# Three passages between blocks of a two-layer transformer, worked through in halves of 256 tokens

## What is computed

```python
h = x
for layer in range(DEPTH):
    u = rmsnorm(h, mix_pre_g[layer])
    ...
        mixed = jnp.concatenate([mla_out, moba_out], axis=-1) @ ab_w_out[e]     # layer 0
    ...
        mixed = stick_breaking_attention(qkv[0], qkv[1], qkv[2]) @ sb_w_out[o]  # layer 1
    h = h + rmsnorm(mixed, mix_post_g[layer])
    u = rmsnorm(h, ffn_pre_g[layer])
    gu = u @ ffn_w_gate_up[layer]
    f = (jax.nn.silu(gu[..., :D_FF]) * gu[..., D_FF:]) @ ffn_w_down[layer]
    h = h + rmsnorm(f, ffn_post_g[layer])
```

## Time and profile before

| | |
|---|---|
| Median of 3 runs | 1420.4 us (1417.37 to 1420.62) |
| The profiled execution's own time | 1417.1 us |
| Its span | 1415.1 us |
| TensorE busy, products (PE) | 1345.1 us, 95% |
| VectorE (DVE) | 728.1 us, 51% |
| ScalarE (ACT) | 528.5 us, 37% |
| GpSimd (POOL) | 239.1 us, 17% |
| Mean granted TensorE clock | 0.974 of full |

### The profile page before, as it was taken

How to read it: one execution, slowest core, us unless ns; L and a number is a source line. 1 busy time by engine, 2 the same in 40 slices (tenths; PEclk the granted TensorE clock), 3 DMA queues, 4 the chain that set the end, 5 groups by cost and what they waited for, 6 DMA issues and landing times.

```text
span 1415.1 us, 16882 instructions
## 1 busy us (share of the span) xinstructions
PE 1345.1 (95%) x6255; PEld 1099.5 (78%) x6255; DVE 728.1 (51%) x925; ACT 528.5 (37%) x796; POOL 239.1 (17%) x156
## 2 busy tenths in 40 slices
PE   7888999988999999999888999999989999999997
PEld 5666888866888888888667888888768888888886
DVE  5777645437544544222366666655376544553223
ACT  5366655544332223222343443333433232223112
POOL 0333000013111111000111222222232111110002
PEclk9989999998999999999898999999979999999999
DMA  5321332131333333333221121120313333333331
GB/s 161 108 52 31 82 82 75 33 102 45 108 100 93 100 94 95 95 94 95 62 60 31 45 60 44 44 74 16 104 45 104 89 104 89 104 105 89 92 102 60
DMA packets 187213, 112.08 MB, mean 79 GB/s; under 512 B 8944, under 2 KB 181557, under 8 KB 187166
## 3 DMA queue, kind: packets, MB, share of 16 engines
q1 hardware_dynamic: 185356, 106.68, 25.9%
q0 software_dynamic: 640, 2.10, 0.5%
q10 hardware_dynamic: 1170, 2.66, 0.5%
HBM read 109.30 MB, written 4.74 MB: 81 GB/s over the span
## 4 chain that ended last, share of the span: by engine, by line
PE 85%; DVE 6%; ACT 3%; issue 3%; POOL 3%; DMA 0%; POOLq 0%; ACTq 0%; DVEq 0%; SPq 0%
PE banks L370 27%; PE banks L372 26%; PE banks L371 26%; PE banks L1382 3%; DVE w_lo L365 1%; POOL residual L606 1%; PE banks L1190 1%; PE banks L403 1%; DVE tf L571 1%; ACT u_hi L594 1%; ACT probsT_hi L1198 0%; DVE logits L1152 0%; PE banks L391 0%; DVE tf L1077 0%; DVE diag L421 0%
## 5 line engine op out<-in xcount | busy, mean ns | idle before, releaser
L365 DVE TENSOR_TENSOR w_lo<-w_raw,w_hi 128x1024 fp32r<-128x1024 f32 (+2 forms) x200 | 298.1, 1493 | 298.6 <-ACT w_hi L358 298.1
L370 PE MATMUL banks<-u_hi,w_hi 128*128 128x512 f32 x1040 | 417.6, 402 | 26.0 <-DVE u_lo L560 21.3
L371 PE MATMUL banks<-u_lo,w_hi 128*128 128x512 f32 x1040 | 411.0, 395 | 0.0
L372 PE MATMUL banks<-u_hi,w_lo 128*128 128x512 f32 x1040 | 410.7, 395 | 0.0
L358 ACT ACTIVATE w_hi<-w_raw 128x1024 fp32r<-128x1024 f32 (+2 forms) x200 | 206.3, 1032 | 247.3 <-PE banks L372 247.2
L370 PEld LDWEIGHTS banks<-u_hi,w_hi 128*128 128x128 f32 x1040 | 198.6, 191 | 78.6 <-issue 20.0
L372 PEld LDWEIGHTS banks<-u_hi,w_lo 128*128 128x128 f32 x1040 | 198.6, 191 | 42.5
L371 PEld LDWEIGHTS banks<-u_lo,w_hi 128*128 128x128 f32 x1040 | 199.0, 191 | 41.2 <-issue 1.0
L693 POOL TENSOR_TENSOR up<-up,gate 128x512 f32<-128x512 f32 x44 | 72.6, 1649 | 400.8 <-DVE up L717 364.0
L677 ACT ACTIVATE gate<-gate 128x512 f32<-128x512 f32 x44 | 27.9, 634 | 214.9 <-DVE gate L713 214.9
L1402 POOL TENSOR_TENSOR stick_lo<-stick,stick_hi 128x1280 fp32r<-128x1280 f32 x16 | 56.7, 3543 | 209.2 <-DVE stick_hi L1398 209.2
(11 more groups left out here) (235 smaller groups left out, 1939.1 us busy)
## 6 DMA issues: line engine op xcount, KB each, us to landing
w_raw<-in_ffn_w_gate_up_dram SPq DMA_DIRECT2D x88, 512.0 KB, 3.8
w_raw<-in_ffn_w_down_dram SPq DMA_DIRECT2D x30, 512.0 KB, 3.6
w_raw<-in_sb_w_qkv_dram SPq DMA_DIRECT2D x24, 512.0 KB, 3.9
w_raw<-in_ab_w_in_dram SPq DMA_DIRECT2D x17, 512.0 KB, 3.9
w_raw<-in_ffn_w_down_dram SPq DMA_DIRECT2D x16, 448.0 KB, 3.6
w_raw<-in_ab_w_out_dram SPq DMA_DIRECT2D x8, 512.0 KB, 3.9
w_raw<-in_sb_w_out_dram SPq DMA_DIRECT2D x8, 512.0 KB, 4.1
bias_by_distance<-bias_rows ACTq DMA_DIRECT2D x1, 2560.0 KB
```

The lines of the kernel that those rows point to most:

```text
L365: dve.tensor_tensor(wl[:, c.slot, 0:w], raw[:, c.slot, 0:w], wh[:, c.slot, 0:w].bitcast(F32), ALU.subtract).then_inc(w_lo, 1)
L370: nc.tensor.matmul(o, lh, rh, start=start, stop=False, skip_group_check=True)
L371: nc.tensor.matmul(o, lh, rl, start=False, stop=False, skip_group_check=True)
L372: return nc.tensor.matmul(o, ll, rh, start=False, stop=stop, skip_group_check=True)
```

## The change

The last output tiles of the block in front of a passage are made by halves of 256 tokens: the last three of the two attention output projections (`NSPLIT_OUT = 5` whole tiles stand in front), the last one of the down projection. First all their first halves, then their second halves. Norm, spread, residual, `u_hi` and `u_lo` of the first half are then made beside the products of the second half, and the next block's first three weight chunks (before, two) are multiplied half by half in `first_products`. The scaling reads the spread's bank for all tiles, and `r_post` is gone. Counts are renumbered: each post-norm has two sets of statistics, and the squares of the new residual have semaphores of their own. The gate-up loops have their first turn written out, with the split of chunk c+5 moved in front of it.

```diff
-        def out_pe(pe, ch, fn, o_at, o_ready, begun):
+        def out_pe(pe, ch, r, fn, k, o_at, o_ready, begun):
             pe.wait_ge(*o_ready)
-            for n in range(KD):
-                if n >= 5:
-                    pe.wait_ge(f_read, fn * KD + n - 4)
+            for n in range(NSPLIT_OUT):
                 out_part(pe, ch, n, o_at, begun[n] if n < len(begun) else 0, KD)
+            for n in range(NSPLIT_OUT, KD):
+                c = Chunk(ch + n)
...
+                half_products(HALF_BANK[n, 0], 0, c, range(KD), 0, KD, o_at).then_inc(half_mm, 1)
+            for n in range(NSPLIT_OUT, KD):
+                c = Chunk(ch + n)
+                if n == NSPLIT_OUT:
+                    pe.wait_ge(f_read, F0[fn] + 4)
+                    half_products(HALF_BANK[n, 1], 1, c, range(4), 0, KD, o_at)
+                    stat_pe(pe, k, R_BANK[r][0], (sq_added, AD0[k + 1]), 2 * r + 1, 0)
+                    half_products(HALF_BANK[n, 1], 1, c, range(4, KD), 0, KD, o_at).then_inc(w_used, 1)
+                elif n == NSPLIT_OUT + 1:
+                    half_products(HALF_BANK[n, 1], 1, c, range(2), 0, KD, o_at)
+                    spread_pe(pe, k, R_BANK[r][0], 0)
+                    half_products(HALF_BANK[n, 1], 1, c, range(2, KD), 0, KD, o_at).then_inc(w_used, 1)
...
+            stat_act(act, k, R_BANK[r][0], D, 0)
+            split_hi(act, Chunk(c))
+            for n in (NSPLIT_OUT, NSPLIT_OUT + 1):
+                f_act_half(act, (w_used, Chunk(ch + n).n + 1), HALF_BANK[n, 1], 1, n, AD0[k + 1] + n - NSPLIT_OUT)
...
+            stat_dve(dve, k, None, None, 0)
+            split_lo(dve, Chunk(c))
+            for h in range(2):
+                scaled(h, 0)
+                for n in range(1, KD):
+                    scaled(h, n)
+                    lo(h, n - 1)
+                    if h == 0 and n == 3:
+                        split_lo(dve, Chunk(c + 1))
+                    if h == 0 and n == 5:
+                        stat_dve(dve, k + 1, None, None, 1)
+                lo(h, KD - 1)
+                if h == 0:
+                    split_lo(dve, Chunk(c + 2))
+            for n in range(1, 4):
+                add_h_squares(dve, r, 0, n)
+            split_lo(dve, Chunk(c + 3))
...
+            split_lo(dve, Chunk(c + 4))
+            split_lo(dve, Chunk(c + 5))
...
+            hi(0, 0)
+            split_hi(act, Chunk(c + 1))
+            hi(0, 1)
+            hi(0, 2)
+            last_half(act)
+            hi(0, 3)
+            hi(0, 4)
+            stat_act(act, k + 1, R_BANK[r][1], D, 1)
...
+        def first_products(pe, c, bs, r, k, added):
+            cs3 = [Chunk(c + n) for n in range(3)]
...
+            for kk in range(4):
+                pe.wait_ge(u_ready, u0 + kk + 1)
+                tile(0, kk, 0)
+            stat_pe(pe, k + 1, R_BANK[r][1], (sq_added, added), 2 * r + 2, 1)
+            pe.wait_ge(w_lo, cs3[1].n + 1)
+            for kk in range(4):
+                tile(1, kk, 0)
+            for kk in range(4, KD):
+                pe.wait_ge(u_ready, u0 + kk + 1)
+                tile(0, kk, 0)
+                tile(1, kk, 0)
+                if kk == 5:
+                    spread_pe(pe, k + 1, R_BANK[r][1], 1)
+            pe.wait_ge(w_lo, cs3[2].n + 1)
+            for kk in range(KD):
+                tile(2, kk, 0)
+            for kk in range(KD):
+                pe.wait_ge(u_ready, u0 + KD + kk + 1)
+                for n in range(2):
+                    mm = tile(n, kk, 1)
+                    if kk == KD - 1:
+                        mm.then_inc(w_used, 1)
+            for kk in range(KD):
+                mm = tile(2, kk, 1)
+            mm.then_inc(w_used, 1)
```

More of the change, by code:

```diff
@@ L470, in bass_hybrid_two_layers, with add_h_squares @@
-        AD0 = [sum(t - (2 if j in posts else 1) for j, t in enumerate(tiles_of[:k]) if j) for k in range(11)]
+                    act.wait_ge(hq_added, H_ADDS * r + (KD - 1) * h + n - 2)
+                dst = tf[:, n % 2, half(h)]
+            act.activation(dst, hT[:, n, half(h)], ACT.Square).then_inc(hq_ready, 1)
+        def add_h_squares(dve, r, h, n):
+            dve.wait_ge(hq_ready, 2 * KD * r + KD * h + n + 1)
+            if n > 1:
+                dve.wait_ge(hq_added, H_ADDS * r + (KD - 1) * h + n - 1)
+            nc.vector.tensor_tensor(acc[:, half(h)], acc[:, half(h)], tf[:, n % 2, half(h)], ALU.add)\
+                .then_inc(hq_added, 1)
@@ L530, in out_part, with half_products @@
                 last.then_inc(w_used, 1)
-        def out_pe(pe, ch, fn, o_at, o_ready, begun):
+        def half_products(b, h, c, ks, at, total, o_at):
+            for k in ks:
+                s = slice(k * P, (k + 1) * P)
+                xh, xl = o_at(at + k)
+                mm = mm3(bank(b)[:, half(h)], wh[:, c.slot, s], wl[:, c.slot, s], xh[:, half(h)], xl[:, half(h)],
+                         start=(at + k == 0), stop=(at + k == total - 1))
+            return mm
+        def out_pe(pe, ch, r, fn, k, o_at, o_ready, begun):
@@ new lines, in first_products, with tile @@
+        def first_products(pe, c, bs, r, k, added):
+            cs3 = [Chunk(c + n) for n in range(3)]
+            def tile(n, kk, h):
+                s = slice(kk * P, (kk + 1) * P)
+                return mm3(bank(bs[n])[:, half(h)], wh[:, cs3[n].slot, s], wl[:, cs3[n].slot, s],
+                           uh[:, kk, half(h)], ul[:, kk, half(h)],
+                           start=(h == 0 and kk == 0), stop=(kk == KD - 1))
+            u0 = KD + 2 * KD * r
+            pe.wait_ge(w_lo, cs3[0].n + 1)
+            for kk in range(4):
[23 more added lines that the diff above has]
+            mm.then_inc(w_used, 1)
@@ L678, in tile @@
                 if not first:
-                    split_hi(act, c.later(3))
+                    if not (isinstance(i, int) and n0 == 1):
+                        split_hi(act, c.later(3))
                     hi(n0 - 1, i)
@@ L683, in gu_act @@
             tile(0, 0, True)
-            with act.Fori(0, (KF - 1) // 3) as i:
+            for b in range(1, 4):
+                tile(b, 0)
+            with act.Fori(1, (KF - 1) // 3) as i:
                 for b in range(1, 4):
@@ L722, in gu_dve @@
             tile(0, 0, True)
-            with dve.Fori(0, (KF - 1) // 3) as i:
+            for b in range(1, 4):
+                tile(b, 0)
+            with dve.Fori(1, (KF - 1) // 3) as i:
                 for b in range(1, 4):
@@ L785, in tile @@
                 c = Chunk(ch + 3 * n0, i, 6)
-                for j in range(3 if n0 < KD - 1 else 2):
+                for j in range(3):
                     split_lo(dve, c.later(3 + j))
@@ L791, in dn_dve, with dn_pool @@
             tile(KD - 2, 0)
-            tile(KD - 1, 0)
+        def dn_pool(pool, fn, k):
+            for n in range(1, KD - 1):
+                f_pool(pool, fn, n, k)
         BANK_ORDER = (6, 7, 2, 3, 4, 5, 0, 1)
```

338 lines of the change are left out of this document (193 added, 145 removed).

## The result

The changed kernel takes **1407.3 us** (median of 4 runs, 1403.83 to 1408.18) against 1419.6 of the kernel before on the same chip (4 runs, 1417.37 to 1420.62): ratio 0.9911, 95% interval 0.9894 to 0.9927, so 12.4 us less. Forecast were 18.5 us less. The profiled execution took 1407.61 us, its span is 1405.6.

A forecast was written before the change was run, and what follows sets the result against it. TensorE, busy 1345.1 of 1415.1 us, was taken as the bound, losing time only in three passages, 51 us in all. Gains 6.7 + 5.1 + 6.7 = 18.5 from 1420.4 give 1401.9, said 1402; range 1395 to 1409, chance 0.65.

The forecast's parts named there:

- A: First in time of the three passages from the last output product into the new residual's products; forecast gain 6.7 us.
- 1, first new product: Passage A, TensorE: the 8.33 us without a product go; first new product at 18.3 us, not 25.1.
- 3, two half steps: Residual loop in A: two half tiles take 2.4 us, 1.2 each; eight tiles 19.2 us against 19.6 before.
- 4, last u of half 1: Residual loop in A with weight splits and statistics beside it: last u at 39.4 us, before 43.3.
- 5, c+2 done: Tail of A on TensorE: three chunks done at 42.9 us, before 50.2; gain 7.3.
- 6, c+6 begins: Behind A's tail: chunk c+6 waits 1.1 us for its split and begins at 61.9 us, before 68.7.
- C: Third passage in time, same program and durations as A; forecast gain 6.7 us.
- B: Second passage, only the last down tile split; gain 5.1 us, counted at the r_pre copy, from which the attention starts.
- The rival: Clock falls in the passages, mostly costing the tail: gain 4 to 5 us a passage, 1415 in all; chance 0.13.
- Slower since half-width operations cost as much as whole ones: Residual loop: steps up to 2.45 us, up to 13 us lost a passage, 1459; chance 0.06.
- The loop running faster than worked out: Residual loop: splits fall into its gaps, 3 us more gain a passage, about 1392; chance 0.12.
- the change does nothing: Whole passages: bound by the loop, gains eaten by late splits, no change; chance 0.04.

The follow-up runs named there:

- e0_again: The changed kernel run once more with no edit, against the kernel before: 1405.0 us, ratio 0.9907.
- e2_copy_back: The changed kernel with the spread copied to SBUF by halves and read there by tiles 1 to 7: 1411.6 us, ratio 0.9952 to the kernel before.
- e3_early_c6: The changed kernel with the weight split of chunk c+6 made in front of the r_pre copy in A and C: 1402.3 us, ratio 0.9879.
- e5_fill: The changed kernel with 14 unread products of 256 columns before the wait for the fourth residual tile, in all passages: 1403.2 us, ratio 0.9894.
- e6_all: The changed kernel with the splits of c+2 and c+6 made earlier and the 14 unread filling products: 1397.5 us, ratio 0.9846.

## Why the prediction was right, and where it was off

The time lies in the stated range, but 1.7 us from its upper end: 12.4 us were gained where 18.5 were forecast. (The prediction's remark that its range leaves out what is above 1414 and below 1390 does not fit the range of 1395 to 1409 that it states.)

**Right: which part of the kernel gains, and by which mechanism.** The passages gain, and all else stays. Of the working for A, counted from the start of output tile 5 (296.74 in the profile of the change, 293.03 in e0_again):

| step | forecast | change | e0_again |
|---|---|---|---|
| 1, first new product | 18.3 | 18.3 | 18.3 |
| 2, split of c ends | 14.6 | 14.8 | 14.8 |
| 3, two half steps | 2.4 | 2.44 | |
| 4, last u of half 0 | 27.7 | 28.7 | 27.65 |
| 4, split of c+2 ends | 29.4 | 30.4 | 29.35 |
| 4, last u of half 1 | 39.4 | 40.8 | 39.7 |
| 5, c+2 done | 42.9 | 44.6 | 43.5 |
| 6, c+6 begins | 61.9 | 64.4 | 63.3 |

**Right: the prices.** All 48 scalings, all 48 remainders, 42 additions and 48 rounded tiles by source line (min/median/max ns):

```profile
L643 DVE SCALAR_TENSOR_TENSOR tf<-block_out,gains,banks x48: 466/474/481, 311.4 to 1036.8; 128x256 f32<-128x256 f32 x48
```
```profile
L653 DVE SCALAR_TENSOR_TENSOR u_lo<-residual,gains,u_hi x48: 470/484/1048, 313.5 to 1038.7; 128x256 fp32r<-128x256 f32 x48
```
```profile
L716 POOL TENSOR_TENSOR residual<-residual,tf x42: 719/741/917, 312.9 to 1037.4; 128x256 f32<-128x256 f32 x42
```
```profile
L685 ACT ACTIVATE u_hi<-residual,gains x48: 493/508/513, 312.9 to 1038.2; 128x256 fp32r<-128x256 f32 x48
```

Forecast were 0.48, 0.48, 0.70 and 0.50. The scaling never exceeds 481 ns, the remainder, which has its operands in SBUF, goes up to 1048. What the prediction cited from the Trainium skill, "SBUF — State Buffer", on which engine shares which port, that a VectorE instruction with at most one SBUF input does not contend with GpSimd, agrees with the scaling. The 0.42 us of an addition of 256 columns had been read from a subtraction with one operand in a bank; the additions with both in SBUF (L648) take 0.42 to 0.46. The step with an SBUF copy was put at 1.35 and measured 1.38 (e2_copy_back).

**Off: steps 5 and 6, the part behind the loop.** The forecast put c+6 at 61.9; in e0_again it begins at 63.3. Of the 1.4 us, 0.3 are there at the last u, 0.3 more at the end of c+2 and 0.8 over the three chunks behind it. I had read the old side from the trace, with every small gap in it, and built the new side from ideal distances between products and splits. In e0_again, for instance, the row sums behind c+3 push the next product back by 1.2 us where I had 0.9, and chunk c+4 takes 5.6 us (343.21 to 348.81) where I had 5.46. The stall itself was foreseen (1.1; it is 1.04 in A and 1.30 in C) and is no part of the error; e3_early_c6 takes it away. In e5_fill, where the clock stayed full in A and C, they gain 5.2 and 5.5, not 6.7: so 1.5 and 1.2 are this error.

**Off: the clock.** The forecast assumed 1.0 through the passages. There is still a stretch at 1.2 GHz in each: 6.8 us in all three of the first profile, 3.4 in A and 6.8 in B and C of e0_again. In front of each stands the 1.84 us wait at the fourth residual tile, which I had in the steps (the u at 22.3 behind the split of c+1) but did not read as a pause of TensorE. The rival priced the clock at 4 to 5 us a passage and 1415 in the whole, most of it in the tail of half products. The tail ran at full clock (1.00 in the third window of passage A). The cost came by a way that neither the forecast nor the rival had: the row sums of the second half fall into the stretch, VectorE waits for them, and the loop ends up to 1.1 us later (0.8 in C). With the filler in that very wait (e5_fill, e6_all) no passage has a low stretch; in the six profiled executions of the change and its variants without filler every passage has one. The pause brings them about. The Trainium skill, "TensorE: Matmul & The Clock Gate", on oscillation, warns of idle gaps, but of longer ones than this; in these traces the clock fell behind 1.84 us already, and the measurement decides. (The prediction's "mostly at 1.2 GHz" for the kernel before is too strong: 0.77 over 19.56 us is 9 us of it.)

**Off: B, where two errors nearly cancel.** The traces have 4.4 and 4.6 for 5.1, but the forecast counted the gain where r_pre is copied. There it is 2.3 us in both (730.53 for 733.19, less the 0.32 by which that trace was ahead). The clock is 1.1 of what is missing, since in e5_fill it is 3.5; of the other 1.6, some 0.5 are there at the last u of the loop and 1.1 behind it, as in steps 5 and 6. The second error is the sentence that the attention starts from r_pre. Before, it did not: TensorE came to the attention's first score products straight from products of its own, 2.0 us after VectorE had their last operand ready. Now it waits for VectorE. The first line is the kernel before, the second the change:

```profile
738.57 0.50 PE L370 MATMUL banks<-sb_q_hi,sb_k_hi 64*128 64x512 f32 x1
```
```profile
734.08 0.46 PE L379 MATMUL banks<-sb_q_hi,sb_k_hi 64*128 64x512 f32 x1 [0.82 <-DVE sb_k_lo L1482]
```

So this product starts 4.2 us earlier (4.5, less the same 0.32) though r_pre gained only 2.3. That B came out near 5.1 is luck.

The sum: with the clock full in all passages (e5_fill) the gains are 5.2, 6.1 and 5.5, in all 16.8 of the 18.5: A and C too small by steps 5 and 6, B too large. The first profile has 3.5 us less, 13.4: 3.0 of them are the three loops behind slow row sums, the rest lies mostly in the attention behind B. The medians gave 12.4 and, again, 13.9.

**The other rivals.** Slower since half-width operations cost as much as whole ones: GpSimd's half takes 0.74 us against 1.27, a step 1.22, far from the 1.6 at which it turns. The loop running faster than worked out: no, it is the 2.4 a pair to 0.04 us. That the change does nothing: no.

## What to carry to other kernels

Where one engine's product must end before a chain of small steps begins, split the product and the chain by the free dimension and start the chain under the second half: it need not become shorter, and the two parts of this change (halves, and a spread read from where it is made) each gave their share by themselves. Then look at what waits next: here the split that stood behind an idle wait for a copy, and moving it and one other gave 5.7 us more at equal clock. Ask of a pause of TensorE not only what it loses but which small result runs slowly behind it, and who waits for that. And build both sides of a difference in the same way, from rows with their gaps in them or from ideal distances, but not one of each.

## What the runs showed that I had not expected

- The places of the low clock stretches are not a property of the program alone. In nine profiled executions of the change and the experiments, the split taken in front of passage A, which no edit reaches, came 0.1 to 4.9 us later than in the trace of before; in e0_again it was 0.2, in the first profile of the same program 3.9. One profile against one other can be off by that. Landmarks ahead of and behind the edited place take it out. They do not take out where a low stretch falls inside the passage: the loop in A took 22.5 us in one execution of the change and 21.4 in the next.
- What one row had suggested before holds without exception: VectorE with an operand in a PSUM bank never queued behind GpSimd's additions: 48 half and 24 whole scalings, none over 15 ns above its median, while the same scaling from SBUF went from 0.47 to 0.95 us.
